# A decoder step in split fp32: three MLP operands stored in DRAM as high and low parts, the last norm worked through PSUM, and the third input chunk squared earlier

## The reference

```python
def block(x, conv_buf, ret_state, pos, p):
    m, new_buf, S_new = mixer(rms_norm(x, n_mix_pre), conv_buf, ret_state, pos, ...)
    h = x + rms_norm(m, n_mix_post)
    f = jnp.square(jax.nn.relu(rms_norm(h, n_ffn_pre) @ w_up)) @ w_down
    return h + rms_norm(f, n_ffn_post), new_buf, S_new
```

## Time and profile before

| | |
|---|---|
| median of 3 runs | 1613.28 us (1611.11 to 1613.76) |
| the profiled execution | 1612.84 us, span 1609.6 us |
| granted TensorE clock, mean | 0.991 |
| PE busy | 96% of the span |
| DVE, ACT, POOL busy | 59%, 32%, 44% |
| DMA | 169.48 MB, 105 GB/s on average |

### The profile page before, as it was taken

One profiled execution on the slowest core, in us unless ns is written; L12 is line 12 of the kernel. 1 busy time (PEld: TensorE's weight loads), 2 busy tenths in 40 slices (PEclk: granted clock), 3 DMA queues, 4 the chain that ended last, 5 costly groups with the idle time before them and its releaser, 6 DMA issues.

```text
span 1609.6 us, 27801 instructions
## 1 busy us (share of the span) xinstructions
PE 1538.8 (96%) x10948; PEld 1518.4 (94%) x10948; DVE 941.7 (59%) x1192; ACT 509.8 (32%) x697; POOL 708.6 (44%) x508
## 2 busy tenths in 40 slices
PE   5999999999999999999999999999999999999993
PEld 4999999999999999999999899999999999999992
DVE  6899959764384234111242885555557666675856
ACT  4100101331231225000122756544446242434332
POOL 3344444342244222444457464444444445455454
PEclk9999999999999999999999999999999999999996
DMA  5211121113321231111142033644447633334332
GB/s 176 92 46 46 46 60 46 46 56 101 98 92 46 86 105 59 46 46 46 46 151 73 14 128 117 245 150 145 146 145 287 223 126 132 130 124 147 102 136 106
DMA packets 83529, 169.48 MB, mean 105 GB/s; under 512 B 7392, under 2 KB 19424, under 8 KB 81136
## 3 DMA queue, kind: packets, MB, share of 16 engines
q1 hardware_dynamic: 69504, 144.61, 27.3%
q10 hardware_dynamic: 13936, 23.60, 4.4%
HBM read 124.82 MB, written 43.36 MB: 104 GB/s over the span
## 4 chain that ended last, share of the span: by engine, by line
PE 45%; DVE 9%; issue 2%; ACT 1%; DMA 1%; POOL 1%; SPq 0%; DVEq 0%; ACTq 0%
PE ps L976 28%; PE ps L631 13%; PE ps L892 3%; DVE tx_l L419 3%; DVE fx_l L419 2%; PE ps L905 1%; DMA hidden_scratch<-stg_b 1%; DVE fac L2009 1%; DVE fx_l L1875 0%; DVE sum_y L1940 0%; DVE fac L2086 0%; DVE sum_x L1931 0%; POOL h_res L575 0%; DVE fac L2095 0%; DVE fac L2055 0%
## 5 line engine op out<-in xcount | busy, mean ns | idle before, releaser
L541 POOL TENSOR_TENSOR w_h<-raw,zero 128x512 fp32r<-128x512 f32 x130 | 142.6, 1097 | 508.4 <-PE ps L631 386.7
L976 PE MATMUL ps<-tx_h,w_h 128*128 128x258 f32 x960 | 272.9, 284 | 10.0 <-DVE fac L2009 3.9
L976 PE MATMUL ps<-tx_l,w_h 128*128 128x258 f32 x960 | 272.0, 283 | 0.0
L976 PE MATMUL ps<-tx_h,w_l 128*128 128x258 f32 x960 | 271.9, 283 | 0.0
L600 POOL TENSOR_TENSOR w_l<-raw,w_h 128x512 fp32r<-128x512 f32 x120 | 182.1, 1519 | 177.8 <-ACT w_h L1371 177.6
L631 PE MATMUL ps<-xn_h,w_h 128*128 128x344 f32 x1128 | 247.9, 326 | 2.7 <-DVE xn_l L1596 1.7
L631 PE MATMUL ps<-xn_l,w_h 128*128 128x344 f32 x1128 | 241.8, 320 | 0.0
L631 PE MATMUL ps<-xn_h,w_l 128*128 128x344 f32 x1128 | 240.9, 320 | 0.0
L976 PE MATMUL ps<-fx_h,w_h 128*128 128x258 f32 x720 | 204.4, 284 | 7.3 <-DVE fac L2055 4.5
L976 PE MATMUL ps<-fx_h,w_l 128*128 128x258 f32 x720 | 203.3, 282 | 0.0
L976 PE MATMUL ps<-fx_l,w_h 128*128 128x258 f32 x720 | 203.1, 282 | 0.0
(11 more groups left out here) (273 smaller groups left out, 2572.0 us busy)
## 6 DMA issues: line engine op xcount, KB each, us to landing
raw<-wseq_dram SPq DMA_DIRECT2D x264, 256.0 KB, 2.7
hq_g<-hidden_scratch SPq DMA_DIRECT2D x14, 1032.0 KB, 7.9
hidden_scratch<-hq_g SPq DMA_DIRECT2D x8, 1032.0 KB, 5.5
stg_a<-hidden_scratch SPq DMA_DIRECT2D x7, 1032.0 KB, 7.1
stg_b<-hidden_scratch SPq DMA_DIRECT2D x7, 1032.0 KB, 7.9
hidden_scratch<-stg_b SPq DMA_DIRECT2D x6, 1032.0 KB, 5.5
rope<-rope_dram ACTq DMA_DIRECT2D x2, 2064.0 KB, 7.8
h_res<-xT_dram ACTq DMA_DIRECT2D x1, 4128.0 KB, 13.7
```

What stands on the lines that cost most here:

```text
L541: pool.tensor_tensor(hi, raw[:, s, :], zero[:, 0:1].broadcast_to([P, SLOT]), ALU.add).then_inc(w_hi, 1)
L976: out = pe.matmul(ps[:, 2 * n + s, 0:HC], RINGS[q % RING][wa][:, kk * P:(kk + 1) * P], OPS[x][xb][:, QK * kh + kk, at_:at_ + HC], start=(i ...
```

## The change

Four edits.

1. *Steps 2, 3 and 4.* For the quarters of `tx` that these steps read, the split is no longer made at the change of group. At the end of each up unit ACT makes the high part of the three rows 4 to 6 of a hidden unit into a new buffer `quad_h` (`hidden_hi`), DVE overwrites the rows with their low part (`hidden_lo`), and SP stores both (`store_quads`; the high parts go to a new DRAM tensor). At the change of group SP loads them straight into `tx_h` and `tx_l` (`load_quads`), as soon as PE is done with each quarter. Only steps 0, 1, 5 and 6 are still staged and split; the list `SPLIT` says so, and their buffers are now fixed, one for each. The waits for stores are counted apart for the first rows (`stored`) and for the rest (`quads_stored`). The last two up units' hidden rows get places of their own (`hq_c`, `hq_d`, `hq_e`).
2. *Orders.* Staging work and `hidden_sums` stand at other places in ACT's and DVE's streams around the up/down boundary and the changes of group.
3. *The end.* The first half's statistic is made ahead of the last step, not within it; each of DVE's scalings writes into a PSUM bank, and the addition reads it there and writes `fac`, one tile at a time. The output is stored in three pieces for each half.
4. *The start.* `x_square(1)` comes ahead of `x_rms(0)`, and `x_square(2)` ahead of `x_rms(1)`.

```diff
             x_square(0)
+            x_square(1)
             act.wait_ge(c_init, 3)
             x_rms(0)
-            x_square(1)
             x_hi(0)
+            x_square(2)
             x_rms(1)
-            x_square(2)
             x_hi(1)
...
+            def hidden_hi(u):
+                act.wait_ge(t_u, 4 * u + 4)
+                if u:
+                    quads_stored(act, u - 1)
+                act.activation(quad_h[:], hq_rows(u, 4, 7), ACT.Copy).then_inc(u_hi, 1)
...
+            def hidden_lo(u):
+                dve.wait_ge(u_hi, u + 1)
+                dve.wait_ge(t_u, 4 * u + 4)
+                rows = hq_rows(u, 4, 7)
+                dve.tensor_tensor(rows.bitcast(F32R), rows, quad_h[:].bitcast(F32), ALU.subtract).then_inc(u_lo, 1)
...
+            def store_quads(u):
+                g, j = divmod(u, QK)
+                sp.wait_ge(u_lo, u + 1)
+                sp.dma_start(qscr[g, :, :, j, :].rearrange("s p n -> p s n"), quad_h[:].bitcast(F32)).then_inc(st_q[u % 2], 16)
                 sp.dma_start(uscr[g, 3:7, :, j, :].rearrange("s p n -> p s n"), hq_rows(u, 4, 8)
-                             ).then_inc(st_u[u % 2], 16)
+                             ).then_inc(st_q[u % 2], 16)
...
+            def load_quads(g):
+                for u in (QK * g + 2, QK * g + 3):
+                    quads_stored(sp, u)
+                for i in range(2, 5):
+                    x, kh, th = X_OF[i]
+                    sp.wait_ge(pm, step_done(UPV + QK * g - 1, i))
+                    sp.dma_start(tx_h[:, KHALVES[kh], HALVES[th]].bitcast(F32), qscr[g, i - 2]).then_inc(q_ld[i - 2], 16)
+                    sp.dma_start(tx_l[:, KHALVES[kh], HALVES[th]].bitcast(F32), uscr[g, OP_SLOT[i]]
+                                 ).then_inc(q_ld[i - 2], 16)
...
                 evicted(act, v, "e6b")
                 act.activation(hq_rows(u, 2, 4), hq_rows(u, 2, 4), ACT.Relu).then_inc(rl, 1)
                 act.wait_ge(rl, 3 * v + 2)
                 act.activation(hq_rows(u, 2, 4), hq_rows(u, 2, 4), ACT.Square).then_inc(sq_u, 1)
+                if v < UPV - 1:
+                    hidden_hi(u - 1)
                 act.wait_ge(pm, step_done(v, 6))
                 act.activation(two(hq_row(u, 1)), pair(a), ACT.Relu).then_inc(ev_a, 1)
...
+                    if (v, i) == (NV - 1, STEPS - 1):
+                        pe.wait_ge(f_ad, 7)
+                        pe.wait_ge(h_cp, 2)
+                        f_ones(0, True, False, 3)
+                        pe.wait_ge(f_sq, 8)
+                        f_ones(3, False, True, 3).then_inc(f_st, 1)
+                    product(v, i)
...
+            def out_norm(t, m, n, dst):
                 dve.wait_ge(f_rp, t + 1)
...
+                dve.scalar_tensor_tensor(pair(dst), two(fac[:, m, HALVES[t]]), vec[:, V_FPOST + m:V_FPOST + m + 1],
+                                         pair(n), ALU.mult, ALU.mult).then_inc(y_n, 1)
+            def out_residual(t, m, src):
...
+                dve.tensor_tensor(two(fac[:, m, HALVES[t]]), pair(src), two(x), ALU.add).then_inc(y_dve, 1)
```

More of the change, by code:

```diff
@@ L110, in build @@
         xn_l, a_B = place("xn_l", [P, KT, T], F32R)
+        quad_h, _ = place("quad_h", [P, 3, HT], F32R)
+        fac01, a_C0 = place("fac01", [P, 2, T])
         u_ext, a_C1 = place("u_ext", [P, CT, UW])
@@ L304, in build @@
         st_u = [sem("st_u0"), sem("st_u1")]
+        st_q = [sem("st_q0"), sem("st_q1")]
+        u_hi = sem("u_hi")
+        u_lo = sem("u_lo")
+        q_ld = [sem(f"q_ld{i}") for i in range(3)]
         h_sp = sem("h_sp")
@@ L957, in bank_ready, with product @@
                     evicted(pe, v, "e6b" if s else "e6a")
-            def product(v, i, between=None):
+            def product(v, i):
                 q = STEPS * v + i
@@ L980, in product @@
                     out.then_inc(pm, 1)
-                    if between and s == 0:
-                        between()
             def h_stat(t):
@@ L1487, in down_unit @@
                 high(v, 4)
-                if first:
-                    staged(4, 0)
                 if p == 3:
@@ L1498, in down_unit @@
                 high(v, 5)
-                if first:
-                    staged(5, 0)
-                if p == 3:
-                    staged(2)
+                if v == UPV + 2:
+                    hidden_hi(UNITS - 1)
                 if last:
@@ L1940, in last_sum, with staged_lo @@
                 dve.tensor_tensor(sum_y[:], raw[:, 1, :], raw[:, 2, :], ALU.subtract).then_inc(s_op, 1)
-            def staged_lo(n, halves=range(2)):
+            def staged_lo(g, k, halves=range(2)):
                 for half in halves:
-                    dve.wait_ge(c_hi, n + 1)
-                    quad_lo(dve, n % STEPS, staged_h(n), slice(2 * half, 2 * half + 2)).then_inc(c_lo, 1)
+                    dve.wait_ge(c_hi, 4 * g + k + 1)
+                    quad_lo(dve, SPLIT[k], staged_h(k), slice(2 * half, 2 * half + 2)).then_inc(c_lo, 1)
             def h_add(n):
@@ L2030, in down_unit @@
                 add(m2, 1, c, step_done(v, 2), True)
+                if p == 3 and g + 1 < GROUPS:
+                    staged_lo(g + 1, 1, (0,))
+                if v == NV - 2:
+                    fold(2, 0, 2, 2)
+                if v == NV - 1:
+                    fold(6, 4, 2, 2)
+                add(m2, 0, a, step_done(v, 3), True)
+                if v == UPV + 1:
+                    hidden_lo(UNITS - 2)
+                if v == UPV + 2:
+                    hidden_lo(UNITS - 1)
                 if p == 0:
-                    staged_lo(STEPS * g + 5)
+                    staged_lo(g, 3)
@@ L2041, in down_unit @@
[L2041 to L2046 removed]
+                    fold(6, 4, 1, 1)
+                    fold(7, 0, 2, 1)
                 evicted(dve, v, "e4")
@@ L2104, in _ @@
                 down_unit(v)
+            v = NV - 1
+            a, b, c = BANKS[v]
             root_argument(0, 3)
-            out_norm(0, 3)
-            root_argument(1, BANKS[NV - 1][1])
-            out_residual(0)
-            out_norm(1, BANKS[NV - 1][1])
-            out_residual(1)
+            fold(9, 4, 2, 1)
+            out_norm(0, 0, 3, c)
+            out_residual(0, 0, c)
+            dve.wait_ge(pm, step_done(v, 6))
+            f = two(fac[:, KT - 2, HALVES[1]])
+            dve.tensor_tensor(f, pair(a), f, ALU.add).then_inc(ev_d, 1)
+            out_norm(0, 1, 3, c)
+            evicted(dve, v, "e7")
+            out_norm(0, 2, 3, a)
+            out_residual(0, 1, c)
+            out_norm(0, 3, 3, c)
+            out_residual(0, 2, a)
+            root_argument(1, b)
+            out_norm(0, 4, 3, a)
+            out_residual(0, 3, c)
+            out_residual(0, 4, a)
+            out_norm(1, 0, b, 3)
+            out_norm(1, 1, b, a)
+            out_residual(1, 0, 3)
+            out_norm(1, 2, b, c)
+            out_residual(1, 1, a)
+            out_norm(1, 3, b, 3)
+            out_residual(1, 2, c)
+            out_norm(1, 4, b, a)
+            out_residual(1, 3, 3)
+            out_residual(1, 4, a)
 def rope_tables():
```

263 lines of the change are left out of this document (129 added, 134 removed).

## The result

The changed kernel takes 1599.51 us (median of 4 runs, 1599.04 to 1600.1) against 1612.65 us (4 runs, 1611.11 to 1613.76) of the kernel before: a ratio of 0.992, 95% interval 0.9909 to 0.9932. The forecast was 1594 us in a range of 1587.5 to 1603. The profiled execution took 1600.1 us, its span is 1598.1 us, so 11.5 us of the span are gone.

A forecast was written before the change was run, and what follows sets the result against it. The matrix engine (PE), busy 96% of the span, was taken as the bound. Terms +2.1 + 0 + 0 - 12.0 - 9.3 = -19.2 us on 1612.84 gave 1593.6; the runs' median, 0.4 higher, 1594 us; range 1587.5 to 1603.

The forecast's parts named there:

- the likeliest case: Whole kernel: the narrower range of 1591 to 1598 us inside the full forecast range.
- The two gains: Three group boundaries, -12 us, and the tail, -9.3 us.
- rival (b): Boundaries: gain partly kept back by late evictions or late up/down weights, 1603 to 1605 us; chance 0.2.
- Term 1: Start: reordered squares make POOL's adds stretch DVE's low parts, +2.1 us, bounds -3.2 and +3.5.
- rival (a): Start: gains because adds lie under the scaling or the second chunk lands sooner, -3.2 us, 1589; chance 0.2.
- Term 2: Up projection: added copies, subtractions and stores fit into existing slack, 0 us, bounds -0.8 and +4.
- Term 3: Up/down boundary: less splitting, but late weights and operand loads cost 9.0 us again, 0 change, bounds -4 and +5.
- Term 4: Three group boundaries: DVE's evictions come before PE wants them, -12 us, bounds -12.4 and -6.
- Rival (c): Operand loads set the pace: at 250 GB/s 1629 us, a loss below 287 GB/s; chance 0.04.
- Term 5: Tail: earlier statistic and outputs through PSUM avoid stretched DVE and POOL work, -9.3 us, bounds -11 and -6.

The follow-up runs named there:

- start_old: Changed kernel with the start's second and third squares both back in the earlier kernel's order, each directly ahead of the chunk whose root it feeds: 1596.76 us.
- second_old: Changed kernel with only the second square back behind the first chunk's root, the third square staying early: 1597.93 us.
- third_old: Changed kernel with only the third square back behind the second chunk's root, the second square staying early: 1594.46 us.
- boundary: Changed kernel with, in up unit 13, the weights and six loads of operands 2 to 4 ahead of the store wait and operands 5 and 6: 1606.24 us.
- boundary2: Changed kernel with, in up unit 13, weights first, then the store wait and operands 5 and 6, then operands 2 to 4: 1597.73 us.
- both duplications: Changed kernel with DVE's low-part halves for groups two to four made twice: all of them, 1633.41 us, or only step 0's two, 1617.73 us.
- group_k0: Changed kernel with only step 0's two low-part halves made twice on DVE at each of the three group boundaries: 1617.73 us.

## Why the prediction was right, term by term

The time lies in the range, 5.5 us above the value and 1.5 above the likeliest case (1591 to 1598). The two gains were right, the costs at the start and in the up projection too small: by the profile both lie above their upper bounds (+3.5 and +4). The total stayed in the range because the two gains came out nearly as forecast and the range reached to rival (b)'s 1603, not because these two terms were right.

**Term 1, the start, +2.1 predicted.** In the profile +4.6 us at PE's last start wait (51.86 against 47.26), 2.75 by the times of start_old. The chain up to DVE was nearly as forecast: the first chunk's low parts end at 30.5 (31.0 predicted), the scaling at 33.5 (34). The step that was mis-sized is "PE, then working without a gap, reaches the third chunk's sum at 39.1": it came at 41.56, since PE came out of two stops at the lower clock level and worked a window of 6 us at 0.50, with 20 products in it; second_old, with the low parts as late and the clock at 1.00, has 38 in it and the sum at 38.60. The forecast had said of the second chunk's early sum that it "was not its limit"; but with the sum done PE had nothing to fill the wait with. The root behind the sum starts at 42.91 instead of 38.31, 4.6 us later where the forecast had 2.1. And "the root and the DVE chain behind it start 1.2 us later" was taken as the second square's whole effect; by itself that square gains 2.3 us, because the second root (22.66 instead of 25.08) lets the adds fall under the scaling. That was rival (a)'s mechanism; in the profiles the first up product comes 3.2 us earlier in third_old than in start_old, the size of its -3.2. The change didn't get it, because it moved the third square past that place too.

**Term 2, the up projection, 0 predicted.** +5.4 in the profile, over the bound of +4. The work was costed rightly (0.4 us remain when the queue is reordered). The step that failed is that the first weight load "goes out some 6 us later; it has over 10". In the third unit the store's subtraction stood behind the sums of the statistics (it began at 1001.01, with ACT's high part ready at 996.55), the load went out at 1003.80 (991.50 before, or 8.0 later beyond the start's 4.3) and landed 8.14 us later, and PE stopped 1.44 us. And "the store behind the 4 MB save of h is counted without its last four rows (-0.5)" had the wrong sign: the save went out at 1029.78, 9.5 us later than before, unit 4's rows behind it landed at 1048, and their eviction on ACT, PE's weights behind it, were late by 2.5 us.

**Term 3, the up/down boundary, 0 predicted.** -1.0. The causes were right, each in its order: 1.8 us for the first weights, 2.4 for step 3's weights and 2.4 for step 4's operand were forecast, and the stops are 0.78, 1.87 and 2.20 us, the last behind operand 4's load. The expectation of the run called boundary took all three for the weights'; boundary2 shortened the first two only.

**Term 4, group boundaries, -12 predicted.** -11.5, no stop at all in 277 us. PE waited for DVE's evictions there before, and both duplications bring such waits back: DVE's work ahead of an eviction sets it. The first boundary had cost 3.4 us, not the 3.9 that the forecast took from its idle time. Rival (c), slow loads, did not occur: PE waits for no operand in those 277 us.

**Term 5, the tail, -9.3 predicted.** -10.3 + 1.6 = -8.7. Of the 10.3 the PSUM way has 5.9 us by the times and 6.3 by the profiles; the other 4.0 are put down to the earlier statistic by subtraction, not by a run of its own. The last unit's products and stop cost 1.6 instead of 0.7.

**Sum.** 4.3 + 5.4 - 1.0 - 11.5 - 8.7 = -11.5 against -19.2 predicted; 1.2 us more were saved outside the span (2.0 instead of 3.2), which varies from run to run (2.0 to 4.3 us in the changed kernel and the experiments) and is not put down to the change.

What stays open: the start's 4.6 us in the profile against 2.75 us in the times. The profiled execution was the slowest of its four, and the six other profiles with the same start have the first up product 0.3 to 1.4 us earlier; that explains a part. Why the clock fell in the changed kernel's start and not in second_old's is told only by the rows above: busy 3.63 and 6.64 of 8 us before.

## What to carry to other kernels

Where two engines exclude each other, moving an instruction earlier can gain or lose with the same edit: ask what it starts (here POOL's adds) and what lies beside it then, and price a stop of PE with the clock behind it. A delay costs little while PE has other products to do. A store that waits for a result, put ahead of loads in one queue, delays all of them; and a gain ahead of a boundary counts only if what the boundary waits for moves too. An engine that is 58% busy can have 0.2 us of slack where it matters: read it at the eviction, not from the share.

## What was not expected of the hardware

A low part of 1032 columns took 1.22 us at its shortest in unit 17 of the changed kernel; four of them with POOL's weight splits beside took 8.07 us in group_k0, 2.0 us each. Work repeated on DVE cost nearly twice what its shortest row says. After a stretch of 8 us with PE busy for 3.63, the clock was 0.50 for the next 6 us although PE was busy for 5.79 of them. And the queue moved 390 to 400 GB/s over 10 us at the boundary:

```profile
1235.00:1245.00 10.00, 10.00 (x85) 10.00 (x85) 7.67 (x11) 5.77 (x9) 5.57 (x4) 1.00 1.05 391
1245.00:1255.00 10.00, 6.89 (x58) 6.68 (x56) 2.48 (x3) 1.65 (x2) 1.24 (x1) 1.00 1.05 401
```

These are of the kernel called boundary above. The Trainium skill, DMA: Bandwidth & Descriptors, Specifications, gives about 358 GB/s per core, which it works out as a memory stack's 716 GB/s shared by two cores. This kernel runs on one core, and the rows are above that share; the measurement decides; no run here shows what two cores would get.
